# Feed-forward projections with a 512-column matmul for the high weights, halves added on reading, and the norm factor applied by GpSimd

## The reference, cut to what matters

```python
D_MODEL, SEQ, D_FF = 1024, 256, 2816

def rms_norm(x, g):
    y = x * lax.rsqrt(jnp.mean(x * x, axis=-1, keepdims=True) + 1e-6)
    return y * g

def swiglu_ffn(h, w_in, w_out):          # w_in: 1024 x 5632, w_out: 2816 x 1024
    gate, up = jnp.split(h @ w_in, 2, axis=-1)
    return (jax.nn.silu(gate) * up) @ w_out

x = x + 0.5 * swiglu_ffn(rms_norm(x, g), w_in, w_out)
```

## Time and profile before

| | before |
|---|---|
| time, median of 3 runs | 2650.41 us (2641.64 to 2651.55) |
| the profiled execution, span | 2652.8 us |
| PE busy | 2573.4 us, 97% of the span, 23370 matmuls |
| DVE busy | 1748.1 us, 66% |
| ACT busy | 1318.0 us, 50% |
| POOL busy | 74.6 us, 3%, 106 instructions |
| mean granted TensorE clock, share of full speed | 0.992 |
| DMA | 424.27 MB moved, mean 160 GB/s |

### The profile page before, as it was taken

The page is one execution under the profiler, slowest core; times in us unless marked ns, Lnnn a source line. Parts: engine busy times, 40 slices in busy tenths (PEclk is TensorE's granted clock), DMA queues, the critical chain, the costliest instruction groups (busy, mean ns, idle before and its releaser), DMA issues.

```text
span 2652.8 us, 60759 instructions
## 1 busy us (share of the span) xinstructions
PE 2573.4 (97%) x23370; PEld 2508.3 (95%) x23370; DVE 1748.1 (66%) x2814; ACT 1318.0 (50%) x1974; POOL 74.6 (3%) x106
## 2 busy tenths in 40 slices
PE   8998998899999999999999999899999999999999
PEld 7997977899999999989999999899999999999999
DVE  5757566566656757767657757967667566665774
ACT  5544433355545546545535547455455455554653
POOL 0000342000000000000000000000000000000000
PEclk9999999999999999999999999999999999999999
DMA  5654201344555655445654655236656564552564
GB/s 193 202 194 134 96 3 42 112 150 152 194 192 174 204 192 204 146 143 176 201 178 144 210 175 192 73 113 204 205 173 201 191 181 131 151 144 88 190 206 143
DMA packets 114323, 424.27 MB, mean 160 GB/s; under 512 B 12433, under 2 KB 19044, under 8 KB 113796
## 3 DMA queue, kind: packets, MB, share of 16 engines
q1 hardware_dynamic: 105696, 408.99, 46.3%
q10 hardware_dynamic: 8484, 13.30, 2.4%
HBM read 421.12 MB, written 1.12 MB: 159 GB/s over the span
## 4 chain that ended last, share of the span: by engine, by line
PE 91%; DVE 4%; ACT 2%; issue 1%; DMA 0%; ACTq 0%; POOL 0%; SPq 0%; DVEq 0%; POOLq 0%
PE bank L470 21%; PE bank L471 21%; PE bank L472 21%; PE bank L396 5%; PE bank L398 4%; PE bank L397 4%; PE bank L2268 2%; PE bank L1684 1%; PE bank L1659 1%; ACT hi L339 1%; PE bank L451 1%; PE bank L452 1%; PE bank L453 1%; PE bank L1230 1%; PE bank L1668 1%
## 5 line engine op out<-in xcount | busy, mean ns | idle before, releaser
L347 DVE TENSOR_TENSOR lo<-raw,hi 128x1024 fp32r<-128x1024 f32 (+1 forms) x728 | 936.0, 1294 | 396.7 <-ACT hi L339 395.2
L339 ACT ACTIVATE hi<-raw 128x1024 fp32r<-128x1024 f32 (+1 forms) x728 | 784.8, 1106 | 338.9 <-PE bank L398 194.5
L470 PE MATMUL bank<-Hh,hi 128*128 128x256 f32 x3056 | 849.5, 278 | 4.6 <-DVE lo L347 4.5
L471 PE MATMUL bank<-Hl,hi 128*128 128x256 f32 x3056 | 848.8, 278 | 0.0
L472 PE MATMUL bank<-Hh,lo 128*128 128x256 f32 x3056 | 848.7, 278 | 0.0
L470 PEld LDWEIGHTS bank<-Hh,hi 128*128 128x128 f32 x3056 | 577.8, 189 | 6.7 <-DVE lo L347 5.7
L471 PEld LDWEIGHTS bank<-Hl,hi 128*128 128x128 f32 x3056 | 574.7, 188 | 0.0
L472 PEld LDWEIGHTS bank<-Hh,lo 128*128 128x128 f32 x3056 | 574.5, 188 | 0.0
L471 PE MATMUL bank<-Al,hi 128*128 128x256 f32 x1408 | 390.5, 277 | 0.0
L472 PE MATMUL bank<-Ah,lo 128*128 128x256 f32 x1408 | 390.5, 277 | 0.0
L470 PE MATMUL bank<-Ah,hi 128*128 128x256 f32 x1408 | 390.4, 277 | 0.0
(11 more groups left out here) (418 smaller groups left out, 4158.7 us busy)
## 6 DMA issues: line engine op xcount, KB each, us to landing
raw<-in_w SPq DMA_DIRECT2D x600, 512.0 KB, 3.4
raw<-in_w SPq DMA_DIRECT2D x128, 704.0 KB, 4.3
dB<-dil_bias ACTq DMA_DIRECT2D x16, 384.0 KB, 9.4
X<-in_x SPq DMA_DIRECT2D x2, 512.0 KB, 5.4
mem_x<-in_mem ACTq DMA_DIRECT2D x1, 1024.0 KB, 5.0
gWS<-in_ws ACTq DMA_DIRECT2D x1, 1024.0 KB
gBS<-in_bs ACTq DMA_DIRECT2D x1, 1024.0 KB
out_x<-X SPq DMA_DIRECT2D x4, 256.0 KB, 2.6
```

The lines of the kernel that those rows point to most:

```text
L339: act.activation(k.hi[:, q, :w], k.raw[:, q, :w], ACT.Copy).then_inc(k.hi_ready, 1)
L347: dve.tensor_tensor(k.lo[:, q, :w], k.raw[:, q, :w], k.hi[:, q, :w].bitcast(F32), ALU.subtract).then_inc(k.lo_ready, 1)
L470: pe.matmul(out, wh, xh, start=first, stop=False)
L471: pe.matmul(out, wh, xl, start=False, stop=False)
```

## The change

1. **One wide matmul.** The high and low activations are now two halves of one tile (`H2`, `A2`: 128 x 2 x chunks x 256). In the feed-forward blocks the high weights meet both in one matmul of 512 moving columns, which writes the whole bank: the product with the high part in columns 0 to 255, the one with the low part in 256 to 511. Low weights by high activations still add 256 columns into the first half. Other stages keep their three matmuls.
2. **Halves added on reading.** In the input projection DVE's two multiplications with `R` become two reductions, which read the 512 columns of the bank as 256 pairs and add each pair. In the output projection `X` gets two additions from PSUM, one for each half, the second waiting for the first.
3. **The norm factor by GpSimd.** GpSimd multiplies `gate` by `R` before ACT's silu, and `sgate` by `R` after it, which stands for the factor of `up`. ACT's silu waits for the first (`gate_scaled`), DVE's `act32` for the second (`sgate_scaled`).
4. DVE no longer waits for `R` before its first step. The other mixers' tiles are only laid out as halves of one tile.

The diff, cut to its core:

```diff
-        self.Hh = self.at("Hh", 0, [P, NC, T], F32R)
-        self.Hl = self.at("Hl", 8 * KB, [P, NC, T], F32R)
+        self.H2 = self.at("H2", 0, [P, 2, NC, T], F32R)
+        self.Hh, self.Hl = self.H2[:, 0], self.H2[:, 1]
...
-        self.Ah = self.at("Ah", self.A0, [P, FC, T], F32R)
-        self.Al = self.at("Al", self.A0 + 22 * KB, [P, FC, T], F32R)
+        self.A2 = self.at("A2", self.A0, [P, 2, FC, T], F32R)
+        self.Ah, self.Al = self.A2[:, 0], self.A2[:, 1]
...
+    def pe_tile(self, pe, bank, q, kc, both, wide, first, last):
+
+
+        k = self.k
+        wh, wl = (w[:, q, kc * P:(kc + 1) * P] for w in (k.hi, k.lo))
+        xh, xl = both[:, 0, :], both[:, 1, :]
+        out = bank[:, :T]
+        if wide:
+            pe.matmul(bank[:].rearrange("p (a t) -> p a t", a=2), wh, both, start=first, stop=last)
+        else:
+            pe.matmul(out, wh, xh, start=first, stop=False)
+            pe.matmul(out, wh, xl, start=False, stop=False)
+        return pe.matmul(out, wl, xh, start=False, stop=last, skip_group_check=wide)
...
+            if st.per_tile > 1 and wide:
+                n = self.half_n
+                dve.scalar_tensor_tensor(k.X[:, c, :], k.bank[s % RING][:, T:], coef, k.X[:, c, :],
+                                         ALU.mult, ALU.add).then_inc(k.half_added, 1)
+                dve.wait_ge(k.half_added, n + 1)
+                self.half_n += 1
             dve.scalar_tensor_tensor(k.X[:, c, :], k.bank[s % RING][:, :T], coef, k.X[:, c, :],
                                      ALU.mult, ALU.add).then_inc(k.banks_freed, st.per_tile)
...
-        sh.pe_first_stage(pe, self.st_in, late=self.n == 0)
+        sh.pe_first_stage(pe, self.st_in, late=self.n == 0, wide=True)
         done = 2 + FC * self.n
         sh.pe_stage(pe, self.st_out,
-                    lambda kg, kc: (k.Ah[:, kg * WIDE + kc, :], k.Al[:, kg * WIDE + kc, :]),
-                    lambda kg, kc: pe.wait_ge(k.al_ready, done + WIDE * kg + kc + 1))
+                    lambda kg, kc: k.A2[:, :, kg * WIDE + kc, :],
+                    lambda kg, kc: pe.wait_ge(k.al_ready, done + WIDE * kg + kc + 1), wide=True)
...
-        dve.wait_ge(k.rstd_ready, sh.norm_n["dve"])
         if self.keys_now:
+            dve.wait_ge(k.rstd_ready, sh.norm_n["dve"])
             k.dve_done.done(dve.tensor_copy(k.RKV[:], k.R[:]), "kv.r")
...
-                dve.tensor_tensor(k.gate[:, j, :], k.bank[2 * j][:, :T], k.R[:], ALU.mult).then_inc(k.gate_scaled, 1)
+                dve.tensor_reduce(k.gate[:, j, :], self.halves(2 * j), AX.X, ALU.add).then_inc(k.gate_summed, 1)
                 sh.dve_lo(dve, s + RING, 2 * j, ahead)
                 dve.wait_ge(k.slab_used, s + 2)
                 dve.wait_ge(k.a_ready, g + 1)
-                dve.tensor_tensor(k.up[:, j, :], k.bank[2 * j + 1][:, :T], k.R[:], ALU.mult).then_inc(k.banks_freed, 2)
-                dve.wait_ge(k.silu_done, g + 3)
+                dve.tensor_reduce(k.up[:, j, :], self.halves(2 * j + 1), AX.X, ALU.add).then_inc(k.banks_freed, 2)
+                dve.wait_ge(k.sgate_scaled, g + 1)
                 dve.wait_ge(k.banks_freed, RING + s + 2)
                 dve.wait_ge(k.al_ready, g + 1)
                 dve.tensor_tensor(k.act32[:, j, :], k.sgate[:, j, :], k.up[:, j, :], ALU.mult).then_inc(k.a_ready, 1)
...
+    def halves(self, b):
+        return self.k.bank[b][:].rearrange("p (a t) -> p t a", a=2)
+
+    def pool(self, pool):
+
+        k = self.k
+        pool.wait_ge(k.rstd_ready, self.norms)
+
+        def body(i, ahead):
+            for j in range(2):
+                g = FC * self.n + 2 * i + j
+                pool.wait_ge(k.gate_summed, g + 1)
+                pool.tensor_tensor(k.gate[:, j, :], k.gate[:, j, :], k.R[:], ALU.mult).then_inc(k.gate_scaled, 1)
+                pool.wait_ge(k.silu_done, g + 3)
+                pool.tensor_tensor(k.sgate[:, j, :], k.sgate[:, j, :], k.R[:], ALU.mult).then_inc(k.sgate_scaled, 1)
+        run(pool, self.st_in, body)
...
-                if isinstance(b, Rwkv7):
+                if isinstance(b, (Rwkv7, FeedForward)):
```

More of the change, by code:

```diff
@@ L287, in __init__ @@
         self.x_scaled = sem("x_scaled")
+        self.half_added = sem("half_added")
         self.mixer_loads = sem("mixer_loads")
@@ L430, in act_stage, with pe_stage @@
         run(act, st, body, between)
-    def pe_stage(self, pe, st, moving, ready, between=None, after_first=None, late=False, rest=False, chunks_first=False, pair=False):
+    def pe_stage(self, pe, st, moving, ready, between=None, after_first=None, late=False, rest=False, chunks_first=False, pair=False,
+                 wide=False):
         k = self.k
@@ L448, in first_pair @@
                         ready(0, kc)
[L449 to L453, removed]
+                        mm = self.pe_tile(pe, k.bank[q], q, kc, moving(0, kc), wide, kc == 0, last)
                     if last:
@@ L466, in body @@
                         ready(kg, kc)
-                    xh, xl = moving(kg, kc)
-                    wh, wl = (w[:, q, kc * P:(kc + 1) * P] for w in (k.hi, k.lo))
                     first, last = kg == kc == 0, kg == st.per_tile - 1 and kc == st.width - 1
-                    pe.matmul(out, wh, xh, start=first, stop=False)
-                    pe.matmul(out, wh, xl, start=False, stop=False)
-                    mm = pe.matmul(out, wl, xh, start=False, stop=last)
+                    mm = self.pe_tile(pe, k.bank[q - kg], q, kc, moving(kg, kc), wide, first, last)
                 mm.then_inc(k.slab_used, 1)
@@ L481, in by_chunks @@
                         pe.wait_ge(k.banks_freed, st.base + q + 1)
[L482 to L486, removed]
+                    mm = self.pe_tile(pe, k.bank[q], q, kc, moving(0, kc), wide, kc == 0, kc == st.width - 1)
                     if kc == st.width - 1:
@@ L513, in pe_stage, with pe_first_stage, pe_stage_h @@
                 body(i)
[L515 removed]
+    def pe_first_stage(self, pe, st, late=False, pair=False, wide=False):
         self.split_n["pe"] += NC
[L518 to L520 removed]
+        self.pe_stage_h(pe, st, lambda: self.norm(pe, "pe"), late, pair=pair, wide=wide)
+    def pe_stage_h(self, pe, st, after_first=None, late=False, rest=False, pair=False, wide=False):
         k, n = self.k, self.split_n["pe"] - NC
[L523 to L524 removed]
+        self.pe_stage(pe, st, lambda kg, kc: k.H2[:, :, kc, :],
+                      lambda kg, kc: pe.wait_ge(k.h_lo, n + kc + 1), after_first=after_first, late=late, rest=rest, pair=pair, wide=wide)
     def dve_project(self, dve, st, dest, scaled=True, before=None, between=None):
@@ L601, in act_resid, with dve_resid @@
             act.preload_act_table(ACT.Sqrt)
-    def dve_resid(self, dve, st, coef, gain, keys=False):
+    def dve_resid(self, dve, st, coef, gain, keys=False, wide=False):
         k, split = self.k, gain not in UNSPLIT
@@ L2932, in make_blocks @@
         if b.startswith("ffn"):
-            out.append(FeedForward(sh, b, n_ffn, gain, keys_next=b == "ffn5", keys_now=b == "ffn6"))
+            norms = n + 1 + ("rwkv" in flow[:n] and "mem" in blocks)
+            out.append(FeedForward(sh, b, n_ffn, norms, gain, keys_next=b == "ffn5", keys_now=b == "ffn6"))
             n_ffn += 1
```

41 lines of the change are left out of this document (22 added, 19 removed).

## The result

The changed kernel takes 2899.54 us (median of 4 runs, 2896.46 to 2903.81) against 2650.98 for the kernel before on the same chip: ratio 1.0919, 95% interval 1.0881 to 1.0956 (the two medians divide to 1.094, inside it). The profiled execution has a span of 2895.3 us against 2652.8, 242.5 us more. The forecast was 2871 us, range 2835 to 2968.

What follows compares the result with a forecast made beforehand. The prediction took the bound to move from PE to the ring of DVE, GpSimd and ACT. The profiled 2652.8 plus 199 us (input) and 21 (output projections) gave 2873, or 2871 us from the median; range 2835 to 2968.

Steps and rivals of the forecast that it cites:

- The ring binds: Input projections: DVE, GpSimd and ACT waiting on each other set the pace, about 6.7 us a step; chance 0.68.
- Input projections, 199 us: First gate to first output matmul, eight blocks: 909.4 us becomes 1109, 199 us more.
- Output projections, 21 us: Eight output projections: 30 us of PE stall, 9 us saved by wide chunks, together 21 us more.
- a 512-column matmul should take 213.3 + 6.7 = 220: Wide matmul: 220 ns in place of 226.7, a chunk 333.3 ns, 6.7 ns saved.
- The bounds of that step: Wide matmul: the saving lies between 0 and 13 ns.
- The chunks' term: Output projections after the stall: PE is the bound again and 1408 chunks save 9 us.
- The stall: Output projections: PE waits 3.8 us in each block for the last Al, 30 us in all.
- The dearer reduction: Input projection: DVE's reduction takes 0.94 us instead of 0.69, 88 us more, total about 2960; chance 0.13.
- The clash with DVE's low weights: Input projection: GpSimd's second multiplication meets them, 0.5 us later each step, 88 us more, about 2960; chance 0.08.
- The fall of the clock: PE's granted clock falls as PE idles a fifth of the time: 120 us more, about 2990; chance 0.03.
- That PE stays the bound and gains: Whole kernel: PE remains the bound and 28 us are saved, 2623 us; chance 0.03.

Runs made afterwards that it cites:

- the doubled multiplication: Changed kernel with GpSimd's second multiplication done twice, first into a spare tile; one execution, span 2988.0 us.
- the open ring with narrow matmuls: Changed kernel without GpSimd's multiplications, ACT's first-slab high weights ahead of the silu, two 256-column matmuls for the wide one; ratio 1.0014 to the kernel before.
- the narrow pair: Changed kernel with only the wide matmul undone, two 256-column matmuls writing the bank's halves; ratio 1.0831 to the kernel before, span 2887.8 us.
- both with the open ring: Changed kernel without GpSimd's multiplications, ACT's first-slab high weights ahead of the silu; narrow matmuls: ratio 1.0014 to the kernel before, wide: 1.0106.

## Why the forecast was right, point by point

The sum made for the profiled execution was 2873 us and its span was 2895.3. The forecast had the mechanism and the largest term right; 20.5 of the 22 us that were missing lie in the output projections.

**The ring binds: shown.** The reading of the earlier trace rows, that nothing in the step waits for PE and that each added microsecond lengthens it, holds. Taking the multiplications out gave 0.83 us a step back, taking the reductions out 0.54, and lifting the high weights over the silu gave most of the loss back with no arithmetic changed. The step's terms, forecast and measured: reduction 0.69 and 0.685; hand-overs and multiplication 0.90 and 0.86; up to act32 0.27 and 0.27; step 6.68 and 6.62. DVE to POOL took 0.08 us and not the 0.14 of the earlier trace rows; why it is shorter here was not looked into.

**Input projections, 199 us: right in the mechanism, and to the microsecond by luck.** In the last block it was 132.4 us from the first gate to the twenty-first and not 133.6, and from there to the first output matmul 5.59 and not 5.0: 138.0 for 138.6. Five blocks are so, which would make the sum 4 to 5 us too high; the three with the longer steps made up for it. The 5.59 is a wait that the forecast had wrong. It had PE released by the first wide slab's low weights, and they were ready 4.9 us after that gate, as forecast. But PE also waits for a free bank, and `up`, which frees it, stands behind the low weights in DVE's queue and ends 0.59 us after them. In this block PE stood idle there from 2822.94 to 2824.51. It is the same in the middle of a step (low weights end at 2703.85, `up` at 2704.44, PE starts at 2704.55), where it costs nothing, as the ring does not wait for PE.

**Output projections, 21 us forecast, 41.5 measured: the term that was mis-sized.** It is the step "a 512-column matmul should take 213.3 + 6.7 = 220", a chunk 333.3 ns. A wide matmul took 235 and the chunk 353.3 in every unbroken stream of every kernel here. The bounds of that step, 0 to 13 ns saved, excluded a loss, and should not have: the surplus over 106.7 ns was taken for a cost per instruction. But 235 ns is 21.7 over the columns' own 213.3, and a narrow matmul of the slower pace, 117.8 ns, is 11.1 over 106.7: half the columns, half the surplus. At that pace it goes with the columns, and merging two matmuls saves none of it. The kernel before already had a second pace, 62.35 against 60.0 us in two of its eight output projections (and 116.67 against 112.4 in two input windows), and the forecast passed it over. The chunks' term was -9 us; the kernel with the wide output projection alone shows +14.0 (498.7 against 484.7, two blocks of which were slow already), so 23 us too little. The stall was 2.6 to 3.0 us and not 3.8, worth -9 us: PE arrives later by the slower chunks and the 0.6 us above, and the last Al a little sooner. The three blocks at half clock add 3 x 1.5 = 4.6 us. The first chunk of each window and the first behind the stall come 0.08 and 0.10 us late, 1.4 us in all. 23 - 9 + 5 + 1 is 20 for a difference of 20.5.

**A wide matmul's time.** The trace has the wide matmul at 235 ns at a granted clock of 1.00. The Trainium skill ("TensorE: Matmul & The Clock Gate", section "Wait — 56ns, not 53.3ns?") gives a warm matmul its columns at 2.4 GHz plus some 2.5 ns; an estimate by that page is 215.8 ns for 512 columns. The trace does not agree, and the measurement decides: the rule of the Trainium skill and the forecast's term are both too low.

**The rivals.** The dearer reduction did not come: adding pairs that lie 256 apart takes what 512 elements take. The clash with DVE's low weights did not come either, by 0.17 us of air; the doubled multiplication shows that its price would have been about 93 us, as forecast (88). The fall of the clock came in small: not in the input projections (granted clock 1.00 in all eight), where PE has gaps of about a microsecond and is busy for 970.5 of 1108.4 us, 88% of these windows, where the forecast had it idle for a fifth, but after the single stall of 2.6 us in the output projections, in three blocks of eight. That PE stays the bound and gains was out twice over: the ring became the bound, and with the ring open there was nothing to gain.

**What stays open.** Why the stream has two paces, 113.3 and 117.8 ns for 256 columns, what moves it from one to the other, and why the wide form never ran at the faster one. The distance between the halves and the two halves of the bank are ruled out as its cause. No version here beats the kernel before; the nearest, the open ring with narrow matmuls, is not to be told from it (1.0014) and leaves the norm's factor out.

## What to carry to other kernels

Before adding anything to an instruction on the side of the bound engine, walk one turn of the loop through the in-order queues and add up the links: here the ring had 0.18 us of slack in a step of 5.44, and the 0.9 us of work on an idle engine came out as 0.83 us more in every step. Do the same for each wait of the bound engine: the profile names one releaser, and the one that ended last may be another. A gain that is expected from merging two matmuls needs the surplus per instruction and per column told apart, which takes two widths; from one width it is a guess in either direction. If work goes to GpSimd, look at which two-input DVE instruction runs beside it, for whichever comes second waits.

## What the runs showed of the hardware that was not expected

- A wide matmul with its own weight load took 235 ns for 512 columns, a narrow one 113.3 or 117.8 for 256, whether the 512 columns were one run or two.
- Narrow streams have two steady paces at a granted clock of 1.00, 0.340 and 0.353 us for three matmuls, and an input projection that no edit touched ran at one in one kernel and at the other in another. It makes 2.35 us in an output projection and up to 4.5 in an input window. The wide form was only seen at 0.353.
- After a stall of 2.5 to 2.8 us (idle time by the profile) between unbroken streams PE came back at 1.2 GHz in three of eight output projections of the changed kernel, in six with ACT's order changed, in all eight with the narrow pair, in one with GpSimd's multiplications left out, where the stall was shorter (1.93 to 2.31 us from start to start against 2.76), and at 2.4 GHz in the others. In the five kernels without a stall there (the kernel before, both with the wide output projection alone, both with the open ring) the granted clock was 1.00 in all forty.
